# First layer of a two-block sequence model: relative bias added on VectorE, small matmuls issued two by two on row and column tiles

## The reference, cut to what matters

```
# 16 heads of 64; position t sees its own chunk of 64 keys and every earlier one (8 chunks back reach all of 256)
s = einsum(q, k) / sqrt(64) + rel_bias[h, clip(t - key, -128, 128) + 128]
s = where(valid, s, -inf);  p = softmax(s);  o = p @ v;  o_a = o * silu(z_a)
# 64 groups of 16 channels, 64 complex states each:  x_t = Abar x_{t-1} + Bbar u_t,  y_t = Re(C x_t) + D u_t
y = gelu(s5_ssm(u, ...));  o_b = y * sigmoid(y @ w_glu + b_glu) * silu(z_b)
x = x + concat(o_a, o_b) @ w_out
```

## Time and profile before

| what | value |
| --- | --- |
| median of three runs | 2992.8 us (2991.71 to 2994.03) |
| the profiled execution | 2991.52 us |
| its span, first to last instruction | 2989.4 us |
| busy share: PE, VectorE, ScalarE, GpSimd | 97%, 39%, 19%, 7% |
| the eight turns of the pair loop | about 36 us to 484 us of the span |
| one turn | 56.0 us (the read-outs 2 and 3 start at 202.87 and 258.91 us) |
| mean granted PE clock | 0.979 of 2.4 GHz |

### The profile page before, as it was taken

The page is one execution under the profiler, slowest core; times in us unless marked ns, Lnnn a source line. Parts: engine busy times, 40 slices in busy tenths (PEclk is TensorE's granted clock), DMA queues, the critical chain, the costliest instruction groups (busy, mean ns, idle before and its releaser), DMA issues.

```text
span 2989.4 us, 45654 instructions
## 1 busy us (share of the span) xinstructions
PE 2892.5 (97%) x17426; PEld 2582.2 (86%) x17426; DVE 1166.3 (39%) x2784; ACT 562.8 (19%) x1242; POOL 199.3 (7%) x416
## 2 busy tenths in 40 slices
PE   7999999989999999899999999999999998999997
PEld 6787787978888889799999988988888998888897
DVE  4655655530100015544454441111112564444554
ACT  2121121011111111233333320112112001222201
POOL 0100100000000000022222220000000000000000
PEclk9999999999999999999999998899999999999998
DMA  5333332434334343233333324333332444344432
GB/s 198 131 129 105 132 128 71 175 108 140 133 135 139 133 161 136 105 134 118 132 134 126 126 91 184 132 118 117 126 127 71 168 167 150 141 161 154 154 140 99
DMA packets 63025, 398.32 MB, mean 133 GB/s; under 512 B 6656, under 2 KB 13312, under 8 KB 16768
## 3 DMA queue, kind: packets, MB, share of 16 engines
q1 hardware_dynamic: 62976, 397.65, 37.7%
HBM read 395.53 MB, written 2.10 MB: 133 GB/s over the span
## 4 chain that ended last, share of the span: by engine, by line
PE 95%; DVE 2%; issue 1%; ACT 1%; POOLq 0%; ACTq 0%; DVEq 0%; POOL 0%
PE psum L490 51%; PE psum L528 17%; PE psum L499 12%; PE psum L722 2%; PE psum L877 1%; PE psum L590 1%; PE psum L668 1%; PE psum L783 1%; PE psum L600 1%; PE psum L577 1%; PE psum L570 1%; PE psum L513 1%; PE psum L820 1%; PE psum L626 1%; PE psum L625 1%
## 5 line engine op out<-in xcount | busy, mean ns | idle before, releaser
L490 PE MATMUL psum<-h,ring 128*128 128x256 f32 x7168 | 1603.0, 382 | 14.9 <-DVE h L1202 14.3
L490 PEld LDWEIGHTS psum<-h,ring 128*128 128x128 f32 x7168 | 1350.6, 191 | 214.5 <-issue 37.1
L499 PEld LDWEIGHTS psum<-ring,h 128*128 128x128 f32 x3072 | 349.7, 192 | 4.6 <-issue 2.7
L499 PE MATMUL psum<-ring,h 128*128 128x128 f32 x3072 | 351.6, 275 | 0.0
L528 PE MATMUL psum<-mix,ring 128*128 128x128 f32 x1792 | 214.3, 276 | 0.0
L528 PEld LDWEIGHTS psum<-mix,ring 128*128 128x128 f32 x1792 | 207.9, 193 | 0.1
L1312 DVE CUSTOM_DVE_ANT_0 score<-psum,con 128x128 f32<-128x128 f32 (+1 forms) x32 | 10.2, 355 | 328.0 <-PE psum L695 328.0
L528 PE MATMUL psum<-h,ring 128*128 128x128 f32 x1024 | 119.9, 275 | 1.7 <-DVE h L1213 1.4
L528 PEld LDWEIGHTS psum<-h,ring 128*128 128x128 f32 x1024 | 117.0, 192 | 2.1 <-issue 1.6
L431 POOL TENSOR_TENSOR wide_a<-w 128x128 f32<-128x128 f32 x32 | 13.9, 435 | 1141.8 <-DVE w L1562 1141.8
L1596 DVE COPY_PREDICATED small<-con,psum 128x256 f32<-128x256 uint32 x128 | 56.8, 444 | 85.0 <-PE psum L725 56.7
(11 more groups left out here) (360 smaller groups left out, 2865.8 us busy)
## 6 DMA issues: line engine op xcount, KB each, us to landing
ring<-w_out SPq DMA_DIRECT2D x80, 1024.0 KB, 5.3
ring<-w_odd SPq DMA_DIRECT2D x64, 1024.0 KB, 4.9
ring<-w_hgrn SPq DMA_DIRECT2D x64, 1024.0 KB, 4.9
ring<-w_even SPq DMA_DIRECT2D x48, 1024.0 KB, 4.9
ring<-w_nsa SPq DMA_DIRECT2D x48, 1024.0 KB, 4.9
ring<-w_rg SPq DMA_DIRECT2D x40, 1024.0 KB, 4.9
ring<-w_cmp_in SPq DMA_DIRECT2D x8, 1024.0 KB, 4.9
ring<-w_rgg SPq DMA_DIRECT2D x10, 512.0 KB, 5.6
```

The costliest lines, as they stand in the source:

```text
L490: mm = pe.matmul(dst[:, 0:T], tile(ph, n, k), h[:, k, :], start=k == 0, stop=k == KT - 1)
L499: mm = pe.matmul(dst[:, tt * P:(tt + 1) * P], h[:, k, tt * P:(tt + 1) * P], tile(ph, n, k), start=k == 0, stop=k == KT - 1)
```

## The change

VectorE adds the bias to the scores while it takes their row maxima, with a fused instruction that writes the sum into the SBUF tile `score`. The flipped-identity matmuls and the constant `flip` go, and the bias lies in plain query order. The exponentials read `score` instead of PSUM. Drives, scores and read-outs are issued in pairs, whose matmuls alternate between two row tiles or two column tiles. The drives of a pair go to banks 6 and 2. Drives 0 and 1 stand where drive 0 stood; drives 2 and 3 stand after product 5, ahead of read-outs 0 and 1; read-outs 2 and 3 keep their place.

```diff
+DRIVE_BANKS = (6, 2)
...
 # SyncE, the load of slot 6
                     sp.wait_ge(bu_ready, after(4 * i))
+                    sp.wait_ge(m_ready, after(2 * i))
...
-                def drive(t):
-                    pe.wait_ge(bu_used, after(4 * i + t))
+                def drive_two(t0):
+                    pe.wait_ge(bu_used, after(4 * i + t0))
                     for c in range(2):
-                        mm = pe.matmul(bank[6][:, c * T:(c + 1) * T], misc[32 * t:32 * t + 32, c * P:(c + 1) * P],
-                                       uT[32 * t:32 * t + 32, :], start=True, stop=True)
-                    mm.then_inc(bu_ready, 1)
+                        for t in (t0, t0 + 1):
+                            rows = slice(32 * t, 32 * t + 32)
+                            mm = pe.matmul(bank[DRIVE_BANKS[t % 2]][:, c * T:(c + 1) * T],
+                                           misc[rows, c * P:(c + 1) * P], uT[rows, :], start=True, stop=True)
+                            if c == 1:
+                                mm.then_inc(bu_ready, 1)
-                def read_out(t):
-                    pe.wait_ge(state_ready, after(8 * i + 2 * t + 2))
+                def read_two(t0):
+                    pe.wait_ge(state_ready, after(8 * i + 2 * t0 + 4))
                     for c in range(2):
-                        mm = pe.matmul(bank[7][32 * t:32 * t + 32, 0:T], c_in[:, c, 32 * t:32 * t + 32],
-                                       w6[:, t % 2, c, :], start=c == 0, stop=c == 1)
+                        for t in (t0, t0 + 1):
+                            mm = pe.matmul(bank[7][32 * t:32 * t + 32, 0:T], c_in[:, c, 32 * t:32 * t + 32],
+                                           w6[:, t % 2, c, :], start=c == 0, stop=c == 1)
...
-                drive(0)
+                drive_two(0)
                 product(even1, i, 2, bank[0])
-                drive(1)
                 pe.wait_ge(q_ready, after(i + 1))
                 values(even1, i, 3, bank[1])
                 pe.wait_ge(k_ready, after(i + 1))
-                pe.wait_ge(bias_masked, after(i + 1))
-                for e in range(2):
-                    for c0, width, q0 in ((0, P, 0), (P, T, P)):
-                        pe.matmul(dst, qT[qk, q0:q0 + P], kT[qk, 0:width], start=True, stop=False)
-                        mm = pe.matmul(dst, flip, bias[:, T - width:T], start=False, stop=True)
-                    mm.then_inc(s_ready, 1)
-                drive(2)
+                pe.wait_ge(bu_used, after(4 * i + 2))
+                for c0, width, q0 in ((0, P, 0), (P, T, P)):
+                    for e in range(2):
+                        mm = pe.matmul(bank[2 + e][:, c0:c0 + width], qT[qk, q0:q0 + P], kT[qk, 0:width],
+                                       start=True, stop=True)
                 product(even1, i, 5, bank[0])
-                read_out(0)
+                pe.wait_ge(m_ready, after(2 * i + 1))
+                drive_two(2)
+                pe.wait_ge(c_in_ready, after(i + 1))
+                pe.wait_ge(y_used, after(i))
+                read_two(0)
                 pe.wait_ge(v_ready, after(i + 1))
                 product(even1, i, 6, bank[1], 0, 9)
-                drive(3)
                 turn_head(0)
-                read_out(1)
                 product(even1, i, 6, bank[1], 9, 13)
...
-                read_out(2)
-                read_out(3)
+                read_two(2)
...
 # ScalarE
-                    exps(bank[2 + e], prob[:, e, :], ...
+                    exps(score[:, e, :], prob[:, e, :], ...
...
 # GpSimd, before it writes the states of quarter t
-                    g.wait_ge(y_ready, after(4 * i + max(t - 1, 0)))
+                    g.wait_ge(y_ready, after(4 * i + 2 * (t // 2)))
...
 # VectorE
-                    v.wait_ge(bu_ready, after(4 * i + t + 1))
+                    v.wait_ge(bu_ready, after(4 * i + 2 * (t // 2) + 2))
...
                 states(0)
                 states(1)
+                v.wait_ge(bias_masked, after(i + 1))
+                v.wait_ge(e_ready, after(2 * i))
+                v.wait_ge(s_ready, after(2 * i + 2))
+                apart(v)
                 for e in range(2):
-                    v.wait_ge(s_ready, after(2 * i + e + 1))
-                    st.mark(v.tensor_reduce(nmax[:, e, 0:1], bank[2 + e][:, 0:P], AX_X, ALU.max, negate=True))
-                    v.tensor_reduce(nmax[:, e, 1:2], bank[2 + e][:, P:384], AX_X, ALU.max, negate=True)\
-                        .then_inc(m_ready, 1)
+                    bias = ring[:, 6, 512 + e * T:768 + e * T]
+                    for tt, (cols, keys) in enumerate(((slice(0, P), slice(P, T)), (slice(P, 384), slice(0, T)))):
+                        st.mark(v.tensor_tensor_reduce(score[:, e, cols], bank[2 + e][:, cols], bias[:, keys], 1.0,
+                                                       -3e38, ALU.add, ALU.max, stat[:, 0, tt, e:e + 1]))
+                    st.settle()
+                    v.tensor_scalar(nmax[:, e, :], stat[:, 0, :, e], -1.0, None, ALU.mult).then_inc(m_ready, 1)
```

More of the change, by code:

```diff
@@ L68 @@
 CONSTS, N_CONSTS = columns([
-    ("half_pi", 1), ("ident", P), ("flip", P), ("ones", P), ("alibi", 384), ("causal", 384), ("alibi_c", 2 * NCMP),
+    ("half_pi", 1), ("ident", P), ("ones", P), ("alibi", 384), ("causal", 384), ("alibi_c", 2 * NCMP),
     ("seen_c", 2 * NCMP), ("slopes", HEADS), ("time", T), ("level", (LEVELS + 1) * P),
@@ L181, in ccol @@
             return con[:, c + a0:c + a0 + (w - a0 if width is None else width)]
-        ident, flip, ones = ccol("ident"), ccol("flip"), ccol("ones")
+        ident, ones = ccol("ident"), ccol("ones")
         ssq = sb("ssq", [P, T])
@@ L585, in pair @@
                 misc = ring[:, 6, :]
[L587 to L588 removed]
+                def drive_two(t0):
+                    pe.wait_ge(bu_used, after(4 * i + t0))
                     for c in range(2):
[L590 to L602 removed]
+                        for t in (t0, t0 + 1):
[6 more added lines that the diff above has]
+                    pe.wait_ge(state_ready, after(8 * i + 2 * t0 + 4))
+                    for c in range(2):
+                        for t in (t0, t0 + 1):
+                            mm = pe.matmul(bank[7][32 * t:32 * t + 32, 0:T], c_in[:, c, 32 * t:32 * t + 32],
+                                           w6[:, t % 2, c, :], start=c == 0, stop=c == 1)
+                            if c == 1:
+                                mm.then_inc(y_ready, 1)
                 def turn_head(e):
@@ L618, in pair @@
                 pe.wait_ge(k_ready, after(i + 1))
-                pe.wait_ge(bias_masked, after(i + 1))
-                for e in range(2):
-                    qk = slice(64 * e, 64 * e + 64)
-                    bias = misc[:, 512 + e * T:768 + e * T]
-                    for c0, width, q0 in ((0, P, 0), (P, T, P)):
-                        dst = bank[2 + e][:, c0:c0 + width]
-                        pe.matmul(dst, qT[qk, q0:q0 + P], kT[qk, 0:width], start=True, stop=False)
-                        mm = pe.matmul(dst, flip, bias[:, T - width:T], start=False, stop=True)
-                    mm.then_inc(s_ready, 1)
-                drive(2)
-                product(even1, i, 5, bank[0])
-                read_out(0)
+                pe.wait_ge(bu_used, after(4 * i + 2))
+                for c0, width, q0 in ((0, P, 0), (P, T, P)):
+                    for e in range(2):
+                        qk = slice(64 * e, 64 * e + 64)
+                        mm = pe.matmul(bank[2 + e][:, c0:c0 + width], qT[qk, q0:q0 + P], kT[qk, 0:width],
+                                       start=True, stop=True)
+                        if c0:
+                            mm.then_inc(s_ready, 1)
+                product(even1, i, 5, bank[0])
+                pe.wait_ge(m_ready, after(2 * i + 1))
[3 more added lines that the diff above has]
+                read_two(0)
                 pe.wait_ge(v_ready, after(i + 1))
                 product(even1, i, 6, bank[1], 0, 9)
-                drive(3)
                 turn_head(0)
-                read_out(1)
                 product(even1, i, 6, bank[1], 9, 13)
@@ L959, in _ @@
                     s.wait_ge(m_ready, after(2 * i + e + 1))
-                    exps(bank[2 + e], prob[:, e, :], [nmax[:, e, t:t + 1] for t in range(2)],
+                    exps(score[:, e, :], prob[:, e, :], [nmax[:, e, t:t + 1] for t in range(2)],
                          [psums[:, e, t:t + 1] for t in range(2)]).then_inc(e_ready, 1)
@@ L1402, in _ @@
             with v.Fori(0, PAIRS) as i:
-                st.enter(i, 48)
+                st.enter(i, 50)
                 st.mark(v.tensor_copy(cur[:, 0:4], s5[:, 0, ds(4 * i, 4)]))
@@ L1407, in _ @@
                 v.wait_ge(landed[6], even1.loads[4].land0 + i * even1.loads[4].land_per)
-                st.mark(v.memset(ring[64:P, 6, 512 + 192:768], NEG))
-                v.memset(ring[64:P, 6, 768 + 192:1024], NEG).then_inc(bias_masked, 1)
```

(9 more changed lines are left out.)

## The result

The changed kernel takes 2943.96 us (median of four runs, 2941.84 to 2944.70), beside 2993.36 us for the kernel before on the same chip. The ratio is 0.9835, with a 95% interval of 0.9818 to 0.9852. The change makes the kernel 1.65% faster.

The account below looks back on a forecast made before the run. PE was taken to bound the eight turns; savings of 1.24 + 4.34 + 0.18 = 5.76 us a turn, 45.6 in all after the last turn's 0.5, took 2991.5 to 2945.9, forecast as a 2947 us median, range 2940 to 2968.

Parts of the forecast that it names:

- PE was the bound, and every piece that went was won: Eight turns: a turn is as long as PE's pieces, so each removed piece is won until another engine's chain is longer.
- Drive 1: Between product 2 and values: removing the drive (1.06 us) and the switch back (0.18) saves 1.24 us a turn.
- The second drive is free: At drive 0's place: the pair on two row tiles costs 1.06 us, nothing more than one drive.
- rival 1: Drives and scores: row tiles take turns, saving 3.4 us a turn (2966 us), at worst 1.4 (2982 us); chance 0.14.
- The estimate of 1.53 times for two tiles: Paired row tiles: speedup in proportion from four tiles' 3.07 times, putting the sum near the partial-overlap case.
- Scores: Scores, flipped-identity matmuls and drive 2: 5.24 us go, 0.9 us of paired scores replace them, saving 4.34 us a turn.
- VectorE's share: Score maxima on VectorE: at most 2.5 us to the last maximum, hidden behind product 5's 7.10 us, costing nothing.
- Product 5 to the end of the turn: PE's pieces shrink 1.3 us, but the chain from states(2) to GpSimd's last addition (17.62 us) limits the gain to 0.18.
- The last turn: Eighth turn: PE already waits 5.5 us for GpSimd, so it loses 0.32 instead of gaining 0.18, 0.5 us less.
- rival 2: Drives and scores: half of each second tile hidden, 1.2 us a turn less saved, 2956 us; chance 0.09.
- rival 4: Whole kernel within 0.2%: rival 1's worst end plus an unseen wait of some 1 us a turn, about 2989 us; chance 0.03.
- rival 3: Ahead of read-outs 2 and 3: the new 1 us wait and narrow tiles drop the clock every turn, 3003 us; chance 0.03.

Follow-up runs that it names:

- the one with the bias alone: Kernel before with the bias on VectorE and both heads' scores on two row tiles, drives and read-outs left single: 2962.7 us, ratio 0.9906.
- on one tile: Changed kernel with both drives of a pair on the rows of the first: 2958.1 us.
- the one with the pairs alone: Kernel before with drives and read-outs paired in their new places, bias still added by TensorE with the flipped identity: 2973.2 us, ratio 0.9940.
- the order with the angles last: Changed kernel with VectorE's states(3) right behind states(2) and the next turn's angles after y: 2931.7 us, ratio 0.9799.
- The kernel before with VectorE's new order: Kernel before with states(3) right behind states(2) and the next turn's angles after y, nothing else changed: 2985.84 us, ratio 0.9978.

## Why the prediction was right, and where a term was off

**PE was the bound, and every piece that went was won.** This held. The turn lost 6.06 us, where the sum had 5.76.

**Drive 1.** Forecast 1.24 us. Drive and values, 1.06 + 7.34, became 7.14. The 7.34 is the chain's piece for values in the kernel before and in the one with the bias alone, where drive 1 stands ahead of values. That is 1.26.

**The second drive is free.** Taken by the nearest rows, two column tiles, and right: 8 records in 1.06 us, and 1.92 on one tile. But one premise was wrong. The prediction calls read-outs 2 and 3 "two tiles fed in turn" and holds "the same alternating order" against rival 1. In the kernel before, read_out(2) issues both its matmuls and read_out(3) then both of its own, and the products with v also go head by head. So those rows showed nothing of alternating tiles. The mistake cost nothing, since the order does not matter for the drives either (1.07 us one after the other). The 1.6 us that rival 1 has at worst came from no row; on one tile the second drive cost 0.86.

The page on array packing in the Trainium skill (TensorEngine Tiling (Array Packing), Key Properties) agrees with the trace: different tiles multiply in parallel, and going from product to drive and back still costs time. A product behind a drive takes 7.10 us, 0.17 above its own records, and values take 7.34 behind a drive and 7.14 behind a product. The estimate of 1.53 times for two tiles, worked out in proportion from the 3.07 times for four in the Trainium skill's TensorE: Matmul & The Clock Gate (Measured speedup vs the span model), did not hold for the drives, since the second costs nothing that the trace resolves.

**Scores.** Forecast 5.24 - 0.9 = 4.34 us; it was 5.24 - 0.86 = 4.38.

**VectorE's share.** It hides, as forecast. The timeline has the fused instructions from 207.68 and the end of the last maximum at 209.28, which is 1.6 us. Once the probabilities are divided by their sums, VectorE idles for 3.80 us ahead of gz:

```profile
207.68 0.29 DVE L1456 CUSTOM_DVE_ANT_0 score<-psum,ring 128x128 f32<-128x128 f32 x1 [2.65 <-PE psum L628]
...
207.90 0.42 DVE L1456 CUSTOM_DVE_ANT_0 score<-psum,ring 128x256 f32<-128x256 f32 x1
...
209.11 0.17 DVE L1459 TENSOR_SCALAR nmax<-stat 128x2 f32<-128x2 f32 x1
```

**Product 5 to the end of the turn.** This is the term that was mis-sized: 0.18 us forecast, 0.42 measured (258.91 - 239.87 = 19.04 before, 233.10 - 214.48 = 18.62 after). The mechanism was right: states(2) starts 1.21 us after product 5 instead of 0.86, and PE waits for the states (0.82 us, "about 1 us" forecast). The step that failed is the chain "From states(2) through the angles, the gate and states(3)", with its 17.62 us and "no wait of PE's in it". It did have one. After the change the same chain, to the end of GpSimd's last addition, is 233.04 - 215.69 = 17.35 us. In the kernel before, the gate of product 6 (L1460) came right behind ScalarE's tanh, which waited for PE:

```profile
250.31 1.22 DVE L1397 SCALAR_TENSOR_TENSOR wide_a<-wide_a,wide_b 128x1024 f32<-128x1024 f32 x1
...
251.10 0.38 ACT L968 ACTIVATE sq<-psum 128x256 f32<-128x256 f32 x1 [0.81 <-PE psum L490]
...
251.65 0.42 DVE L1460 SCALAR_TENSOR_TENSOR mix<-sq,psum 128x256 f32 x1
```

L1460 starts 1.34 us after L1397. In the changed kernel, where product 6 is done earlier, L1470 starts 1.13 us after L1401. The 0.21 us are most of the 0.24 us that the term was short. The profile doesn't name this short wait, so it is read from the distances, but the kernels with one part each bear it out. In the one with the pairs alone, where product 6 is early too, the distance is 1.13 to 1.14 us in all eight turns. In the one with the bias alone it is 1.32 to 1.33, and in the kernel before 1.33 to 1.34.

PE's own pieces of this stretch were sized rightly. Forecast 17.73 us; in the order with the angles last, where PE bounds it, it takes 229.74 - 212.01 = 17.73.

The terms of the measured turn add up: 1.26 + 4.38 + 0.42 = 6.06 us.

**The last turn.** Forecast to win 0.5 us less than the others, and it did: 5.5 against 6.06. The clock was low there before and after, for about as long behind the read-outs (from 433.00 to about 439 us, before from 482.52 to about 488.7).

**Outside the loop.** The 1.6 us ahead of the first drive were not forecast. The first drive starts at 41.29 us in the changed kernel and at 42.49 in the kernel with the other order, whose program up to there is the same. Over the profiles of this study it lies anywhere between 40.60 and 42.91. It goes with how long the clock was low between 24 and 31 us (granted 0.53 before, 0.76 after). The nine profiles with 0.76 start at 40.60 to 41.48 us, the four with 0.51 to 0.57 at 41.93 to 42.91. The kernel before with VectorE's new order, whose program up to there is that of the kernel before, has 0.76 and starts at 40.68. So I count it as chance and not as the change's. The forecast for the profiled execution was 2945.9 us and it took 2941.84: of these 4.1 us, 2.3 lie in the loop and 1.8 outside, where they are luck.

**The rivals.** Taking turns (rival 1) and partial overlap (rival 2) fall with the drives of 1.06 us and the scores of 0.86. A change within 0.2% (rival 4) falls with the time, and the loop has no other wait of PE's. The clock in every turn (rival 3) falls too, since it is granted in full over a whole turn with the new wait in it:

```profile
182.00:232.00 50.00, 49.18 (x280) 41.00 (x278) 32.59 (x77) 10.21 (x21) 5.71 (x9) 1.00 0.40 136
```

## What to carry to other kernels

Small matmuls on different row tiles are worth placing side by side. For two tiles that write to different banks the second drive was free, in whichever order the pair was issued; one bank for both, and three or four tiles, were not tried. Each block of another tile shape that disappears saves its switch as well, here about 0.2 us. When PE is the bound and its work shrinks, follow the next engine's chain through the stretch before counting on the rest. Here 0.8 us of each turn and more of the last went into a wait for VectorE, and moving the six microseconds of the angles out of that chain, with states(3) ahead of the gate, brought 12 us back.

A chain taken over as fixed should be searched for waits that the shrinking engine itself releases: such a wait shrinks with it.

## What was not expected of the hardware

The time outside the changed loop moved by up to 5 us between kernels whose code there is the same: 2506.9 us from the last wait of the loop to the end in the kernel before, 2511.6 in the kernel with the pairs alone. Mean granted clocks went with it, 0.979 and 0.976. Such a difference also comes without any change of code: over the comparisons of this study the kernel before took 2988.4 us at a mean granted clock of 0.980 and 2995.9 at 0.976. What decides how long such a low stretch lasts was not tested.
